# Spreading the gather and scatter of routed experts over the steps between them in a two-block transformer kernel

## What the reference computes

```python
def moe_swiglu(h, w_router, w1, w3, w2):
    logits = jnp.einsum("btd,de->bte", h, w_router).astype(jnp.float32)
    top_v, top_i = lax.top_k(logits, TOP_K)            # TOP_K = 2 of 8 experts
    gates = jax.nn.softmax(top_v, axis=-1)
    combine = jnp.sum(jax.nn.one_hot(top_i, N_EXPERTS) * gates[..., None], axis=-2)
    out = jnp.zeros_like(h)
    for e in range(N_EXPERTS):
        out = out + combine[..., e:e + 1] * swiglu(h, w1[e], w3[e], w2[e])
    return out                                          # swiglu: (silu(h w1) * (h w3)) w2
```

## Time and profile before

| | us |
|---|---|
| median of 3 runs | 2358.5 |
| lowest, highest | 2358.09, 2366.73 |
| profiled execution | 2362.61 |
| its span, first to last instruction | 2360.8 |
| TensorE busy in the span | 2032.1 (86%) |
| VectorE busy | 1749.4 (74%) |
| ScalarE busy | 1173.1 (50%) |
| mean granted TensorE clock | 0.93 of full |

### The profile page before, as it was taken

One profiled execution on the slowest core, in us unless ns is written; L12 is line 12 of the kernel. 1 busy time (PEld: TensorE's weight loads), 2 busy tenths in 40 slices (PEclk: granted clock), 3 DMA queues, 4 the chain that ended last, 5 costly groups with the idle time before them and its releaser, 6 DMA issues.

```text
span 2360.8 us, 28658 instructions
## 1 busy us (share of the span) xinstructions
PE 2032.1 (86%) x11392; PEld 1742.5 (74%) x11392; DVE 1749.4 (74%) x1985; ACT 1173.1 (50%) x1350; POOL 61.7 (3%) x96
## 2 busy tenths in 40 slices
PE   1677899886679999999999999968978998977999
PEld 1666798775567777777777777747858997966998
DVE  4778888885767878787878787878767887776454
ACT  0452433344246666666666666644544434544443
POOL 3001000000000000000000000000000000000000
PEclk9999899888779999999999999988978999987999
DMA  9454699743448989898989898965516996422552
GB/s 320 137 175 164 228 347 342 270 137 125 143 137 301 326 290 337 283 339 285 317 305 327 295 326 306 317 214 179 174 52 223 339 331 235 146 72 90 179 192 94
DMA packets 366381, 554.40 MB, mean 235 GB/s; under 512 B 12860, under 2 KB 303920, under 8 KB 366240
## 3 DMA queue, kind: packets, MB, share of 16 engines
q1 hardware_dynamic: 362256, 544.10, 66.8%
q0 software_dynamic: 3552, 8.29, 1.2%
q10 hardware_dynamic: 432, 0.11, 0.0%
HBM read 551.40 MB, written 1.05 MB: 234 GB/s over the span
## 4 chain that ended last, share of the span: by engine, by line
PE 63%; DVE 21%; ACT 8%; issue 4%; DMA 2%; POOL 0%; SPq 0%; DVEq 0%; ACTq 0%; POOLq 0%
PE bank L408 19%; PE bank L409 19%; PE bank L410 19%; DVE ring_lo L1597 5%; ACT ring_hi L1030 3%; DVE acc L1562 3%; PE bank L903 1%; DMA ring<-in_ada_w_dram 1%; PE bank L850 1%; PE bank L436 1%; DMA ring<-in_ffn_w_dram 1%; DVE work L1746 1%; ACT work L1148 1%; PE bank L864 1%; DVE XN L1799 1%
## 5 line engine op out<-in xcount | busy, mean ns | idle before, releaser
L1597 DVE TENSOR_TENSOR ring_lo<-ring,ring_hi 128x2048 fp32r<-128x2048 f32 x421 | 961.9, 2287 | 262.4 <-ACT ring_hi L1030 262.1
L1030 ACT ACTIVATE ring_hi<-ring 128x2048 fp32r<-128x2048 f32 x421 | 801.6, 1906 | 299.7 <-PE bank L410 134.5
L408 PE MATMUL bank<-hh,ring_hi 128*128 128x256 f32 x1152 | 335.3, 291 | 28.4 <-DVE ring_lo L1597 15.7
L409 PE MATMUL bank<-hl,ring_hi 128*128 128x256 f32 x1152 | 331.5, 288 | 0.0
L410 PE MATMUL bank<-hh,ring_lo 128*128 128x256 f32 x1152 | 331.5, 288 | 0.0
L408 PE MATMUL bank<-ring_hi,hgh 128*128 128x512 f32 x704 | 292.5, 416 | 1.4 <-DVE hgl L2194 1.2
L408 PE MATMUL bank<-ring_hi,hh 128*128 128x256 f32 (+2 forms) x704 | 236.5, 336 | 56.1 <-DVE ring_lo L1597 22.7
L409 PE MATMUL bank<-ring_lo,hgh 128*128 128x512 f32 x704 | 281.2, 399 | 0.0
L410 PE MATMUL bank<-ring_hi,hgl 128*128 128x512 f32 x704 | 280.9, 399 | 0.0
L1562 DVE SCALAR_TENSOR_TENSOR acc<-ring,csil,acc 128x1024 f32<-128x1024 f32 x192 | 246.2, 1283 | 43.8 <-DMA ring<-in_ada_w_dram 27.8
L408 PE MATMUL bank<-ring_hi,uh 128*128 128x512 f32 x616 | 248.7, 404 | 14.2 <-DVE ul L2214 13.0
(11 more groups left out here) (346 smaller groups left out, 2444.8 us busy)
## 6 DMA issues: line engine op xcount, KB each, us to landing
ring<-in_moe_w_dram SPq DMA_DIRECT2D x352, 512.0 KB, 5.0
ring<-in_moe_w_dram SPq DMA_DIRECT2D x88, 1024.0 KB, 6.1
ring<-in_ada_w_dram SPq DMA_DIRECT2D x48, 1024.0 KB, 7.6
ring<-in_w_mod_dram SPq DMA_DIRECT2D x48, 1024.0 KB, 7.5
ring<-in_w_in_dram SPq DMA_DIRECT2D x40, 1024.0 KB, 5.4
ring<-in_ffn_w_dram SPq DMA_DIRECT2D x33, 1024.0 KB, 6.0
ring<-in_w_gate_dram SPq DMA_DIRECT2D x22, 1024.0 KB, 5.3
ring<-in_w_up_dram SPq DMA_DIRECT2D x22, 1024.0 KB, 5.4
```

The lines of the kernel that those rows point to most:

```text
L408: pe.matmul(ps, xh, wh, start=first, stop=False)
L409: pe.matmul(ps, xh, wl, start=False, stop=False)
L1030: act.activation(ring_hi[i % NH][:, 0:z], ring[n % NS][:, 0:z], ACT.Copy).then_inc(*s.hi(("hi", home(s, i), i)))
L1597: dve.tensor_tensor(ring_lo[n % NS][:, 0:z], ring[n % NS][:, 0:z], hi, ALU.subtract).then_inc(*s.lo(("lo", home(s, i), i)))
```

## The change

The once-per-expert work is cut into pieces, and the pieces are put at other places of the loop:
- TensorE: `gather(e + 1)` in halves at i = 7 and i = 8, `scatter(e - 1)` by token tile at i = 4 and i = 5. `gates(e)` stays at i = 2.
- VectorE: `SG` of `gates(e)` at the end of `up` in step 1; the evictions of the scatter in steps 5 and 6, between `ul` and block A's low part; the places `ga_S` at the end of `up` in step 6; the second half of the gather and the low part of the first in step 9, the low part of the second in step 10, both behind that step's `U`.
- ScalarE: `GT` behind the silu of step 3; the first half of the gather behind the silu of step 8, the high part of the second behind that of step 10.

On TensorE:

```diff
-                def gather(e):
-                    for half in range(2):
+                def gather(e, half):
...
-                gather(0)
+                gather(0, 0)
+                gather(0, 1)
                 for j in range(89):
...
-                    if i == 4 and 1 <= e < 8:
-                        scatter(e - 1)
-                    if i == 7 and e < 7:
-                        gather(e + 1)
-                scatter(7)
+                    if i in (4, 5) and 1 <= e < 8:
+                        scatter(e - 1, i - 4)
+                    if i in (7, 8) and e < 7:
+                        gather(e + 1, i - 7)
+                scatter(7, 0)
+                scatter(7, 1)
```

On ScalarE, the added lines in `up(j)` behind the silu, the removed ones at the end of the loop:

```diff
+                    if i == 3:
+                        gates(e)
+                    if i == 8 and e < 7:
+                        first_half(e + 1)
+                    if i == 10 and e < 7:
+                        second_half(e + 1)
...
-                    if i == 2 and e < 8:
-                        gates(e)
-                    if i == 7 and e < 7:
-                        gather(e + 1)
```

On VectorE:

```diff
-                def gather(e):
+                def places(e):
...
+                def second_half(e):
...
+                def low_half(e, half):
+                    z = slice(4 * half, 4 * half + 4)
+                    dve.wait_ge(*at("few", "hgh", e, half))
+                    dve.tensor_tensor(hgl[:, e % 2, z, :], hg[:, e % 2, z, :], hgh[:, e % 2, z, :].bitcast(F32), ALU.subtract).then_inc(*s.vec(("few", "hg", e, half)))
...
                     if j:
                         turn(j - 1)
+                    if i in (5, 6) and e:
+                        scatter(e - 1, i - 5)
                     low_halves(s, min(turn_of["moe", e, "w13", i, 1] + 2, moe1))
...
+                    if i == 1:
+                        gates(e)
+                    if i == 6 and e < 7:
+                        places(e + 1)
+                    if i == 9 and e < 7:
+                        second_half(e + 1)
+                        low_half(e + 1, 0)
+                    if i == 10 and e < 7:
+                        low_half(e + 1, 1)
...
-                    if i == 2 and e < 8:
-                        gates(e)
-                    if i == 4 and 1 <= e < 8:
-                        scatter(e - 1)
-                    if i == 7 and e < 7:
-                        gather(e + 1)
-                scatter(7)
+                scatter(7, 0)
+                scatter(7, 1)
```

More of the change, by code:

```diff
@@ L840, in moe_picked @@
                 s = few
-                def gather(e):
-                    for half in range(2):
[L844 to L851, removed]
+                def gather(e, half):
+                    ps = psum("gather", e, half)
+                    if half == 0:
+                        pe.wait_ge(*at("few", "S", e))
+                    for k in range(4):
+                        kc = 4 * half + k
+                        for t in range(2):
+                            x = pe.matmul(ps[:, 128 * k:128 * k + 128], XN[:, t, 128 * kc:128 * kc + 128], ga_S[:, e % 2, t, :], start=t == 0, stop=t == 1)
+                    x.then_inc(*s.small(("few", "gathered", e, half)))
                 def gates(e):
@@ L894, in down, with scatter @@
                     x.then_inc(*s.prod(("few", "down", j), ("use", "few", ("moe", e, "w2", i))))
[L896 to L904, removed]
-                gather(0)
+                def scatter(e, t):
+                    for h in range(2):
+                        ps = psum("scatter", e, t, h)
+                        if t == 0 and h == 0:
+                            pe.wait_ge(*at("few", "y", e))
+                            pe.wait_ge(*at("few", "GT", e))
+                        x = pe.matmul(ps[:, :], GT[:, e % 2, 128 * t:128 * t + 128], ysb[:, e % 2, 512 * h:512 * h + 512], start=True, stop=True)
+                        x.then_inc(*s.small(("few", "scattered", e, t, h)))
+                gather(0, 0)
+                gather(0, 1)
                 for j in range(89):
@@ L1387, in moe_picked, with first_half @@
                 s = few
-                def gather(e):
+                def first_half(e):
                     ps = R.of("gather", e, 0)
@@ L1434, in down @@
                         x.then_inc(*s.act(("few", "y", e)))
-                gather(0)
+                first_half(0)
+                second_half(0)
                 for j in range(89):
@@ L1443, in moe_picked @@
                         down(j - 1)
-                    e, i = divmod(j, 11)
-                    if i == 2 and e < 8:
-                        gates(e)
-                    if i == 7 and e < 7:
-                        gather(e + 1)
             for r0, nm in ((0, "c"), (8, "c_2")):
@@ L2192, in gather, with second_half @@
                     x.then_inc(*s.vec(("few", "S", e)))
-                    dve.wait_ge(*at("few", "hgh", e, 0))
-                    dve.tensor_tensor(hgl[:, e % 2, 0:4, :], hg[:, e % 2, 0:4, :], hgh[:, e % 2, 0:4, :].bitcast(F32), ALU.subtract).then_inc(*s.vec(("few", "hg", e, 0)))
+                def second_half(e):
                     dve.wait_ge(*at("few", "gathered", e, 1))
@@ L2201, in gather @@
                     x.then_inc(*s.vec(("few", "hg1", e), ("free", "gather", e, 1)))
-                    dve.wait_ge(*at("few", "hgh", e, 1))
-                    dve.tensor_tensor(hgl[:, e % 2, 4:8, :], hg[:, e % 2, 4:8, :], hgh[:, e % 2, 4:8, :].bitcast(F32), ALU.subtract).then_inc(*s.vec(("few", "hg", e, 1)))
+                def low_half(e, half):
+                    z = slice(4 * half, 4 * half + 4)
+                    dve.wait_ge(*at("few", "hgh", e, half))
+                    dve.tensor_tensor(hgl[:, e % 2, z, :], hg[:, e % 2, z, :], hgh[:, e % 2, z, :].bitcast(F32), ALU.subtract).then_inc(*s.vec(("few", "hg", e, half)))
                 def gates(e):
@@ L2230, in down, with scatter @@
                     low_halves(s, min(turn_of["moe", e, "w2", i] + 2, moe1))
[L2232 to L2244, removed]
+                def scatter(e, t):
+                    for h in range(2):
+                        c, ps = slice(512 * h, 512 * h + 512), R.of("scatter", e, t, h)
+                        dve.wait_ge(*at("few", "scattered", e, t, h))
+                        if e == 0:
+                            x = dve.tensor_copy(YK[:, t, c], ps[:, :])
+                        else:
+                            dve.wait_ge(*at("free", "scatter", e - 1, t, h))
+                            x = dve.tensor_tensor(YK[:, t, c], YK[:, t, c], ps[:, :], ALU.add)
+                        x.then_inc(*s.vec(("free", "scatter", e, t, h)))
+                places(0)
+                low_half(0, 0)
+                second_half(0)
+                low_half(0, 1)
                 for j in range(89):
```

## The result

The changed kernel takes 2293.66 us (median of 4 runs, 2292.5 to 2295.82), the kernel before 2359.45 beside it: ratio 0.9716, 95% interval 0.9695 to 0.9738. The forecast was 2293.4.

What follows compares the result with a forecast made beforehand. TensorE was taken to set the pace in the routed layer, standing 48.3 us at three places. Waits 47.3, restarts 3.5 and slow clock 20.6 removed, 6.3 added: net 65.1, against the median 2358.5 giving 2293.4 us, range 2285 to 2309.

Steps and rivals of the forecast that it cites:

- All three kinds: TensorE's routed-layer waits to go: 19.3 us before the gates' transposes, 16.0 before the gather, 12.0 of 13.0 for ul.
- 0.16 of restart: TensorE's extra loss at each wait besides its length; 22 waits go, 3.5 us together.
- The slow clock: Twelve-product groups and gathers at halved clock behind waits, about 1.6 us extra each; 7.6 + 6.5 + 6.5 = 20.6 to go.
- The new wait: TensorE in up(10) waits 0.74 us for block B's low part, delayed by VectorE's gather work in step 9; 5.2 us over seven.
- the sum: Forecast total: 71.4 us removed, 6.3 added, net 65.1; profiled execution 2362.6 to 2297.5, median 2293.4.
- more changes of kind: First product behind transposes or gathers comes 0.08 us later; 14 more such places, 1.1 us added.
- Cost nothing: Half scatters in steps 5 and 6: the two evictions, 1.2 us, end before block A's high part arrives, adding no time.
- if the cover were gone, 1.2 each time would meet a spare of 0.8: Steps 5 and 6: without TensorE's half-scatter pause, 1.2 us of evictions would eat into block A's 0.8 us spare.
- Gather on ScalarE: Step 8: first half delays block B; its low part ends 2.25 into step 9, needed at 2.80, hidden by TensorE's half gather.
- The forecast of 1.2: Stall in us predicted for ScalarE's step 8 gather work if TensorE's half gather did not cover it.
- Loads: Weight loads average 336 GB/s at 103 us per expert; no cost taken, 7 x 1 us as the other bound.
- those named as wrong: Profile signs against the forecast: ring_lo waits in steps 0, 6 or 9, ScalarE waiting for loads, slow stretches without long waits.

Runs made afterwards that it cites:

- gates_only: Kernel before with only SG moved behind U of step 1 and GT behind the silu of step 3; 2334.27 us, ratio 0.9868.
- early_only: Kernel before with SG written early in step 1 (GT in step 3) and ga_S in step 6, nothing split; 2315.62 us, ratio 0.9793.
- gates_back: Changed kernel with only the gates put back, SG again behind block B's low part at the end of step 2; 2319.79 us, ratio 0.9808.
- places_back: Changed kernel with only the places ga_S put back to VectorE's end of step 7; 2316.78 us, ratio 0.9816.
- thin_scatter: Changed kernel with TensorE's scatters of experts 0 to 6 multiplying 128 of 512 columns, VectorE's evictions whole; 2278.51 us, ratio 0.9646.
- thin_half: Changed kernel with TensorE multiplying one of four column blocks of the gather's second half, experts 1 to 7; 2292.65 us, ratio 0.9701.

## Why the prediction was right

**The waits that go.** All three kinds behaved as priced. gates_only, early_only, gates_back and places_back each moved the layer by its own waits and 0.16 of restart each, and no new kind of wait turned up. The slow clock did not keep to its places: behind the waits for `ul` there are 4 slow groups before, 5 in gates_only and 7 in early_only, and these waits grew from 13.0 to 13.5 and 14.2 us.

**The new wait.** Forecast in the middle of `up(10)` of seven experts, at 0.74; found there at 0.63. Step 9 ran as walked: `U` 7.73 into the step counted from 1066.88 (7.65 said), block B's low part at 9.94 (9.87 said). The step itself was 8.70 long where 8.62 was said, so this low part ended 3.53 into step 10, as forecast (3.54). What made the wait 0.1 cheaper is the signal: the sum allows 0.14 from the end of a low part to the product that needs it, and here the product starts 0.04 to 0.06 behind the row's end (1079.11 and 1079.15).

**What was mis-sized.** The layer gained 68.0 where the sum has 65.1. The new wait was 7 x 0.63 = 4.4 for 5.2. The 1.1 for more changes of kind was not there. Counted up to the second product behind them, less one usual spacing, a half scatter takes 1.72 and a whole one 3.43, and a half gather 1.78 and a whole one without a wait 3.57 (early_only): two halves cost what the whole does. A whole gather behind the wait for `ga_S` took 3.65, so 7 x 0.08 = 0.6 more went with these waits. Together 2.5 of the 2.9.

**The scatter.** "Cost nothing" holds. "if the cover were gone, 1.2 each time would meet a spare of 0.8" counts too much: thin_scatter showed no wait, and only 0.5 of the 1.2 meet that spare, because 0.7 fall into VectorE's own idle time before block A.

**Gather on ScalarE.** Hidden, as said, and only by the half gather: thin_half brought 0.65 a time in step 9. The forecast of 1.2 was for all of the passes gone; here 0.4 of them were left.

**Loads.** 338 GB/s over the layer (336 forecast), share 0.99, no wait of ScalarE for a load. Over the 88 such loads of the page, 1 MB took a median of 6.1 us to land, as before. Over step 10 to the next gather, one expert's stretch, it was 5.9:

```profile
ring<-in_moe_w_dram SPq DMA_DIRECT2D x11, 1024.0 KB, 5.9
```

**The slow clock.** The 20.6 us did go, all of them, and none came with the new wait. That these groups come and go by themselves was known only roughly, see below.

**The signs.** None of those named as wrong turned up: no wait on a `ring_lo` in steps 0, 6 or 9, and no stretch of the layer at half clock. An expert takes 102.8 us (103 said).

**Luck.** The median was met to 0.3 us partly by luck. The layer gained 68.0, 2.9 more than the sum, but the medians differ by only 65.8, since the stretches ahead of the layer and behind it vary by a few us on their own. The profiled execution took 2292.50, where the sum has 2297.5 for it.

## What to carry to other kernels

A small instruction queued behind a long one of the same engine can cost the pacing engine far more than its own length: here two matrices of some 0.5 us each, written once per expert behind a 2.29 us split instead of before it, cost some 47 us with all that followed. Before work is spread out, look at where each piece stands against the long instructions; that order gave two thirds of the gain, the spreading one third, and splitting the scatter, whose evictions already ran beside TensorE's own passes, gave nothing. Write down each engine's starts within one plain step, with what is to spare before TensorE wants it: such numbers predicted where the new wait would be, and later that the idle stretch between `ul` and block A would take part of the work that caused it.

## What was not expected of the hardware

The length of a wait does not alone decide whether the clock halves behind it. Behind waits of 2.41 us before the gates it did 5 times of 8 in the kernel before, and 2 of 8 in gates_back, where the gathers no longer waited. Behind the waits of 1.88 in early_only it did 7 times of 7; those stand a few us behind a whole gather of short passes. Behind the waits of 2.29 before the gather it did 4 times of 7 in the kernel before and 3 of 7 in places_back. Among the waits for `ul` alone, in the kernel before, gates_only and early_only, length and clock do go together: all 16 of 1.81 to 1.89 us were followed by a slow group, none of the five of 1.27 to 1.74. But all five shorter ones came behind a gather that was itself at half clock, so length may not be the cause. Two windows of gates_back, both behind a wait of 2.42, one with the drop and one without:

```profile
917.77:921.90 4.13, 4.13 (x14) 3.23 (x13) 1.53 (x1) 2.18 (x2) 0.00 (x0) 0.67 0.46 183
1024.30:1028.50 4.20, 4.20 (x21) 3.43 (x22) 1.62 (x1) 3.00 (x4) 0.00 (x0) 1.00 0.50 200
```

The waits of 0.40 in step 10 never brought it in any run. What decides between the two cases was not settled; no run here was made for it alone.
